# Moving the 1/rms factor of the feed-forward norm behind the gate product, and building the first operands inside the output projection

## The reference

```
h = x + jnp.concatenate([att, y], axis=-1) @ w_out
f = rmsnorm(h, norm_ffn)          # h * (1/rms(h)) * g, 1/rms is one number per token
h = h + (jax.nn.silu(f @ w_gate) * (f @ w_up)) @ w_down
```

## Time and profile before

| | |
|---|---|
| median of 3 runs | 2945.24 us (2944.84 to 2957.09) |
| profiled execution | 2950.53 us, of which the span of the trace is 2948.7 us |
| PE | 2762.0 us busy (94%) |
| DVE | 1696.8 us busy (58%) |
| ACT | 1022.3 us busy (35%) |
| POOL | 391.4 us busy (13%) |
| mean granted TensorE clock | 0.975 |

### The profile page before, as it was taken

One profiled execution on the slowest core, in us unless ns is written; L12 is line 12 of the kernel. 1 busy time (PEld: TensorE's weight loads), 2 busy tenths in 40 slices (PEclk: granted clock), 3 DMA queues, 4 the chain that ended last, 5 costly groups with the idle time before them and its releaser, 6 DMA issues.

```text
span 2948.7 us, 49257 instructions
## 1 busy us (share of the span) xinstructions
PE 2762.0 (94%) x20329; PEld 2628.2 (89%) x20329; DVE 1696.8 (58%) x2517; ACT 1022.3 (35%) x1517; POOL 391.4 (13%) x166
## 2 busy tenths in 40 slices
PE   7999998999999988996899999999999989999997
PEld 7977998877777766995899999999999989999997
DVE  3222699345444445106777777777766787777423
ACT  5233221333323233223433433343344353443222
POOL 2322332211111101341000000000000000000231
PEclk9999999999999998997999999999999999999999
DMA  6322322655555546341334334333432364654521
GB/s 236 95 83 66 102 80 67 167 158 156 149 154 151 155 121 211 126 132 47 102 118 132 119 110 131 126 110 121 136 102 96 128 223 155 222 162 159 197 102 65
DMA packets 394447, 388.80 MB, mean 132 GB/s; under 512 B 25405, under 2 KB 354725, under 8 KB 391160
## 3 DMA queue, kind: packets, MB, share of 16 engines
q1 hardware_dynamic: 367112, 360.00, 38.9%
q10 hardware_dynamic: 27120, 25.77, 2.6%
HBM read 319.11 MB, written 68.00 MB: 131 GB/s over the span
## 4 chain that ended last, share of the span: by engine, by line
PE 72%; issue 14%; DVE 5%; POOL 5%; ACT 2%; DMA 1%; SPq 0%; ACTq 0%; POOLq 0%; DVEq 0%
PE PS L1335 43%; PE PS L890 16%; PE PS L1317 5%; POOL WL L782 4%; PE PS L1085 1%; PE PS L1282 1%; PE PS L1269 1%; PE PS L1056 1%; PE PS L1075 1%; PE PS L1113 1%; DVE xo_t L2466 0%; PE PS L1259 0%; POOL WL L815 0%; PE PS L1102 0%; DMA xin<-in_x_prompt 0%
## 5 line engine op out<-in xcount | busy, mean ns | idle before, releaser
L1335 PE MATMUL PS<-xo_t,WH 128*128 128x288 f32 x2560 | 519.5, 297 | 21.7 <-ACT kept L1745 10.0
L890 PE MATMUL PS<-AH,WH 128*128 128x288 f32 (+1 forms) x2208 | 490.2, 304 | 19.8 <-POOL WL L782 6.4
L890 PE MATMUL PS<-AL,WH 128*128 128x288 f32 (+1 forms) x2208 | 478.7, 299 | 0.0
L890 PE MATMUL PS<-AH,WL 128*128 128x288 f32 (+1 forms) x2208 | 477.6, 298 | 0.0
L1335 PEld LDWEIGHTS PS<-xo_t,WH 128*128 128x128 f32 x2560 | 414.9, 190 | 23.4 <-issue 23.4
L1335 PE MATMUL PS<-xo_x,WH 128*128 128x288 f32 x1920 | 387.2, 296 | 14.7 <-DVE xo_x L2432 14.3
L890 PEld LDWEIGHTS PS<-AH,WH 128*128 128x128 f32 (+1 forms) x2208 | 361.5, 192 | 42.1 <-issue 34.4
L1335 PE MATMUL PS<-xo_t,WL 128*128 128x288 f32 x1280 | 379.6, 297 | 0.0
L890 PEld LDWEIGHTS PS<-AL,WH 128*128 128x128 f32 (+1 forms) x2208 | 361.9, 192 | 0.0
L890 PEld LDWEIGHTS PS<-AH,WL 128*128 128x128 f32 (+1 forms) x2208 | 361.0, 191 | 0.0
L2318 DVE TENSOR_TENSOR WL<-WRAW,WH 128x1024 fp32r<-128x1024 f32 x200 | 244.7, 1224 | 138.7 <-ACT WH L1737 137.6
(11 more groups left out here) (369 smaller groups left out, 3606.1 us busy)
## 6 DMA issues: line engine op xcount, KB each, us to landing
WRAW<-in_w_gate SPq DMA_DIRECT2D x22, 2048.0 KB
WRAW<-in_w_up SPq DMA_DIRECT2D x22, 2048.0 KB
WRAW<-in_w_down SPq DMA_DIRECT2D x32, 1024.0 KB
WRAW<-in_w_in SPq DMA_DIRECT2D x14, 2048.0 KB, 8.3
raw<-in_w_in SPq DMA_DIRECT2D x48, 512.0 KB, 4.1
kca<-in_cache_k SPq DMA_DIRECT2D x256, 64.0 KB, 2.8
vca<-in_cache_v SPq DMA_DIRECT2D x256, 64.0 KB, 2.0
WRAW<-in_w_out SPq DMA_DIRECT2D x16, 1024.0 KB, 10.9
```

Of the source, the lines that this page charges most:

```text
L890: last = nc.tensor.matmul(G[gslot][0:width, h, 0:HALF], wt[:, half if slot is None else slot, k % 8, 0:width], act[:, k, h * HALF:(h + 1) ...
L1335: last = mm(out, wt[:, k, :], act[:, m, k, :], start=(j in (0, 1, 3) and k == 0 and wt is wh and m == 0), stop=(k == 7 and wt is wl), skip ...
```

## The change

- **1/rms.** `XR` is no longer multiplied by 1/rms. The seven products run on h*g. The sums of the gate pair in `gs2` are multiplied by 1/rms before silu (`scale_gate(.., False)`), and the result of silu is multiplied by it again (`scale_gate(.., True)`), which stands for the factor of the up sums. That is four DVE multiplications of 128x576 for each of 22 gate/up couples, placed at the preparation of j = 3 (one), 4 (one) and 5 (two) of the odd pair; `gates` on ACT moves one product later. The sum of squares now accumulates in `rstd` itself. `norm_sum` moves on PE from ahead of product 0 to ahead of product 4, the two roots on ACT behind `cast(6)`, and the reciprocal becomes two of 128x288 on DVE at steps 6 and 7.
- **Operands.** The residual is added in `xt`, which is squared, stored and weighed from there. x00 and the difference t1 are made after tile 8, t3 and t2 tile by tile (`pieces`, two DVE operations of 128x288). The seven operands lie at other addresses, so that x00 can be written while the output projection still reads its own operands. `load_x` on SP now waits for the store, the square and the weighing of tile n-2.
- **Order.** Pair 0 does its products in the order j = 0, 3, 1, 2, 4, 5, 6. The second of the three weight slots is the separate buffer `W3`, so both the first and the second weight operand are made before the last half unit ends.
- **End of the Strassen part.** DVE makes the four low parts `low_hidden(0, 0, j)` ahead of its last two `gather`s, and PE waits for all sums only before the second half of its first down product.

```diff
-              (("x00", low), ("x10", low + SET), ("t1", low + 2 * SET), ("t2", low + 3 * SET), ("x11", high), ("t3", high + SET), ("t4", old))}
+              (("x10", low), ("t2", low + SET), ("t1", low + 2 * SET), ("x11", low + 3 * SET), ("x00", high), ("t3", high + SET), ("t4", old))}
+        acc = rstd[:, :, :].rearrange("p a b -> p (a b)")
+        seq[0:7] = [(0, j) for j in (0, 3, 1, 2, 4, 5, 6)]
             def load_x(n):
                 if n >= 2:
-                    sp.wait_ge(s["tile_taken"], T3 + n - 1)
+                    sp.wait_ge(xr_st[n % 2], 16 * (n // 2))
+                    sp.wait_ge(s["sqf_done"], n - 1)
+                    sp.wait_ge(s["x_g"], n - 1)
-            return WH[:, r, :, :] if r < 2 else W3[:, 0, :, :]
+            return W3[:, 0, :, :] if r == 1 else WH[:, r // 2, :, :]
...
+                    if t and isinstance(c, int) and c == CD:
+                        pe.wait_ge(s["e_add"], 4 * NALL)
-            norm_sum()
             for c, (q, j) in enumerate(seq):
+                if c == 0:
+                    pe.wait_ge(s["tile_taken"], T3 + KT)
+                if c == 4:
+                    norm_sum()
...
-                act.wait_ge(s["e_add"], ADD[2 * p, 6])
                 for t in range(2):
+                    act.wait_ge(s["gate_sc"], 2 * p + t + 1)
                     actv(gs2[:, t, :], gs2[:, t, :], ACT.Silu).then_inc(s["p_silu"], 1)
-                if c % 14 == 8 and c // 14 < NPAIR // 2:
+                if c % 14 == 9 and c // 14 < NPAIR // 2:
                     gates(c // 14)
...
+            def pieces(n):
+                k = n - 8
+                x01, x11 = XR[:, k, HALF:NT], XR[:, n, HALF:NT]
+                dve.wait_ge(s["x_g"], n + 1)
+                tt(x01, x11, x01, ALU.subtract).then_inc(s["x_n"], 1)
+                dve.wait_ge(s["x_n"], 2 * k + 2)
+                tt(XR[:, k, 0:HALF], x01, XR[:, k, 0:HALF], ALU.add).then_inc(s["x_n"], 1)
+            def scale_gate(p, t, again):
+                if again:
+                    dve.wait_ge(s["p_silu"], 2 * p + t + 1)
+                else:
+                    dve.wait_ge(s["ry_done"], 3)
+                    dve.wait_ge(s["e_add"], ADD[2 * p, 6])
+                tt(gs2[:, t, :], gs2[:, t, :], acc, ALU.mult).then_inc(s["silu_sc" if again else "gate_sc"], 1)
...
+                    if c in (6, 7):
+                        given(dve, f"ssf{c - 6}")
+                        nc.vector.reciprocal(rstd[:, c - 6, :], rstd[:, c - 6, :]).then_inc(s["ry_done"], 1)
+                    if q2 % 2 and q2 < NPAIR and j2 in (3, 4, 5):
+                        for t in ((0,), (1,), (0, 1))[j2 - 3]:
+                            scale_gate(q2 // 2, t, j2 == 5)
+                    if c == NPROD - 1:
+                        for j in range(4):
+                            low_hidden(0, 0, j)
```

More of the change, by code:

```diff
@@ L383, in build @@
                 RAW[q, what] = len(RAW) + 1
+        RAW[0, "difference"], RAW[0, "sum"] = RAW[0, "sum"], RAW[0, "difference"]
         assert all(POS[q, 6] == max(POS[q, j] for j in range(7)) for q in range(NALL))
@@ L1763, in _ @@
                     hi_p(C3 + c, c % 4, c // 4)
-                if c % 2 and c >= 3:
-                    n = (c - 3) // 2
-                    squares(n)
-                    if n:
-                        weigh_x(n - 1)
-            cast(0, 0, 0, 0, 0)
-            squares(15)
-            weigh_x(14)
-            cast(1, 0, 1, 1, 0)
+                if c % 2:
+                    squares((c - 3) // 2)
+                    weigh_x((c - 3) // 2)
+                if c == 17:
+                    act.wait_ge(s["x_g"], 8)
+                    x_high("x00", x_part(0, 0))
+            cast(0, 0, 0, 0, 0)
+            cast(1, 0, 3, 1, 0)
+            act.wait_ge(s["w_used"], C3 + 32)
+            act.wait_ge(s["x_n"], 1)
+            x_high("t1", diff[:, :, :])
+            weigh_x(15)
+            cast(2, 0, 1, 2, 0)
+            act.wait_ge(s["x_g"], 16)
+            x_high("x10", x_part(1, 0))
+            squares(15)
+            act.wait_ge(s["x_n"], 17)
+            x_high("t2", x_part(0, 0))
+            keep(0, 0, 0)
+            cast(3, 0, 2, 0, 0)
+            keep(0, 3, 0)
+            act.wait_ge(s["x_lo"], 2)
+            x_high("t3", x_part(0, 1))
+            cast(4, 0, 4, 1, 0)
+            x_high("x11", x_part(1, 1))
+            keep(0, 2, 0)
+            cast(5, 0, 5, 2, 0)
+            act.wait_ge(s["x_n"], 18)
+            act.wait_ge(s["x_lo"], 5)
+            x_high("t4", x_part(1, 0))
+            cast(6, 0, 6, 0, 0)
             for h in range(2):
@@ new lines, in pieces @@
+            def pieces(n):
[5 more added lines that the diff above has]
+                tt(XR[:, k, 0:HALF], x01, XR[:, k, 0:HALF], ALU.add).then_inc(s["x_n"], 1)
+            for n in range(KT):
+                if n:
+                    add_squares(n - 1, "sqf_done", "ssf_used")
+                if n == 9:
+                    x_low("x00", x_part(0, 0), 1)
+                    dve.wait_ge(s["x_lo"], 1)
+                    tt(diff[:, :, :], x_part(0, 1), x_part(0, 0), ALU.subtract).then_inc(s["x_n"], 1)
+                    dve.wait_ge(s["x_n"], 1)
+                if n >= 9:
+                    pieces(n - 1)
+                if n == 15:
+                    dve.wait_ge(w_ld[0], 160)
+                    sum_w(0, 1, 0)
+                    low_w(0, 0, 0, 0)
+                    difference(0, 0)
+                    low_w(1, 3, 1, 0)
@@ L2404, in _ @@
                 dve.wait_ge(xt_in[n % 2], 16 * (n // 2 + 1))
                 dve.wait_ge(s["w_used"], C3 + (2 * n + 2 if n else 3))
-                tt(two(XR[:, n, :]), G[(T3 + n) % 2][:, :, 0:HALF], two(xt[:, n % 2, :]), ALU.add).then_inc(s["tile_taken"], 1)
-                if n:
-                    add_squares(n - 1, "sqf_done", "ssf_used")
-                if n == 14:
-                    low_w(0, 0, 0, 0)
-                    difference(0, 0)
-                    second(0, 2, 0)
-            add_squares(KT - 1, "sqf_done", "ssf_used")
@@ L2416, in _ @@
-            low_w(1, 1, 1, 0)
-            fourth(0, 2, 0)
-            for h in range(2):
-                given(dve, f"ssf{h}")
-            nc.vector.reciprocal(rstd[:, :, :], rstd[:, :, :]).then_inc(s["ry_done"], 1)
-            dve.wait_ge(s["ry_done"], 2)
-            def normed(kh, th):
-                dve.wait_ge(s["x_g"], 8 * kh + 8)
-                v = x_part(kh, th)
-                tt(v, v, rstd[:, th, :].rearrange("p (k t) -> p k t", k=1).to_broadcast([P, 8, HALF]), ALU.mult).then_inc(s["x_n"], 1)
@@ L2453, in _ @@
+                tt(two(x), G[(T3 + n) % 2][:, :, 0:HALF], two(x), ALU.add).then_inc(s["tile_taken"], 1)
+            x_low("t1", diff[:, :, :], 2)
+            low_w(2, 1, 2, 0)
+            pieces(15)
+            x_low("x10", x_part(1, 0), 3)
+            add_squares(15, "sqf_done", "ssf_used")
+            prepare(3, 0, 2, 0, 0, lambda: x_low("t2", x_part(0, 0), 4))
+            dve.wait_ge(s["x_lo"], 3)
             tt(x_part(1, 0), x_part(1, 0), x_part(0, 0), ALU.subtract).then_inc(s["x_n"], 1)
-            prepare(5, 0, 5, 2, 0)
+            for t in range(2):
+                dve.wait_ge(xr_st[t], 16 * (KT // 2))
@@ L2455, in _ @@
+            prepare(4, 0, 4, 1, 0, lambda: x_low("t3", x_part(0, 1), 5))
+            prepare(5, 0, 5, 2, 0, lambda: x_low("x11", x_part(1, 1), 6))
             x_low("t4", x_part(1, 0), 7)
```

98 lines of the change are left out of this document (28 added, 70 removed).

## The result

The changed kernel takes 2923.78 us, the median of seven runs (2917.94 to 2938.63); the kernel before, also in seven runs, takes 2949.82. The ratio is 0.9917, with a 95% interval from 0.9901 to 0.9933: 20 to 29 us faster. The forecast was 2914.3, in a range from 2907 to 2923; so the time lies 0.8 us outside. The seven runs of before have a median 4.6 us above that of the three runs from which the forecast started. That explains nearly half of the 9.5 us between forecast and time, and the rest has to be found in the trace. The profiled execution of the changed kernel has a span of 2922.0 us (before 2948.7).

The account below looks back on a forecast made before the run. PE (94% busy) bounds the kernel, its idle time lying at the joints, mostly ended by DVE. -33.1 + 3.7 + 2.0 - 3.5 = -30.9, so 2945.2 becomes 2914.3 us; range 2907 to 2923.

Parts of the forecast that it names:

- rivals 1 and 2: First: clock falls inside pair 0, time 2921, chance 0.12. Second: each odd pair leaks, time 2925, chance 0.09.
- Joint 1: Between output projection and pair 0's end: shorter DVE chain ends pair 0 at 1387.2 for 1420.3, gain 33.1 us.
- Rival 1: Clock falls inside pair 0: products 3 to 6 take 6.4 us each, pair 0 ends 9.6 us later; 2921, chance 0.12.
- Pair 1: Two reciprocals of 1.9 us come when DVE has no lead; PE waits 0.8, 2.1 and 0.8 us, cost 3.7.
- Later odd pairs: Four more DVE steps of 0.68 us per couple; ACT's `keep` of j = 2 has 1.3 us left, cost nothing.
- rivals 2 and 3: Second: odd pairs leak 0.5 us each, 2925, chance 0.09. Third: multiplications are dear (3.75 us each), 3015, chance 0.02.
- Joint 2: At q = 44, where DVE becomes the bound: last couple's multiplications fall directly ahead, cost 2.0 us, bounds 0 and 4.
- Projection: Inside the output projection: 11.8 us more DVE and a 2.11 us cast find room, cost 0; other end 3.9 us.
- Joint 3: End of the Strassen part: low parts go ahead of two gathers, PE's whole 3.47 us wait goes, gain 3.5 us.
- The base: The median of the runs shown, 5.3 us below the profiled execution: 2945.2 us, from which the forecast time was taken.

Follow-up runs that it names:

- r1: The changed kernel itself run again, beside others on the same chip: 2923.9 us, ratio 0.9917 to the kernel before.
- r2: The changed kernel with the load of the second hidden group ahead of the last store of sums, run again: 2920.98 us, ratio 0.9908.
- e1: The changed kernel with SP's load of the second hidden group issued ahead of the last store of sums: 2916.71 us, ratio 0.9883 to the kernel before.
- e2: The changed kernel with the end of the Strassen part in its old order: 2929.7 us, ratio 0.9923 to the kernel before.
- e6: The changed kernel without the multiplications of gate sums and silu by 1/rms, both reciprocals kept: 2920.74 us, ratio 0.991 to the kernel before.
- e6b: The changed kernel without the four 1/rms multiplications of each couple and without the two reciprocals: 2917.22 us, ratio 0.9878 to the kernel before.
- e7: The changed kernel with the first multiplication of each gate half done twice: 2936.34 us, ratio 0.9956 to the kernel before.
- f3: The changed kernel with the early hidden load, and low parts of three pair 0 weights made by POOL, not DVE: 2917.49 us, ratio 0.9892.

## Why the prediction was off

The forecast's sum was -33.1 + 3.7 + 2.0 - 3.5 = -30.9 on the profiled execution. By the landmarks it is -32.8 + 2.7 + 1.7 + 3.1 = -25.3. Another 0.1 us was lost within the down products, and 1.5 were won ahead of T, which other executions give and take back: -26.7 in all. The median lies at 2923.78, near the 2921 and 2925 of rivals 1 and 2; that is chance, for neither is what happened.

- **Joint 1: right, to 0.3 us.** The forecast took DVE's row at 1420.29 as the end of pair 0 before and PE's end as that after; on PE's rows alone its 33.1 are 32.9, and 32.8 were measured. PE's idle times of 0.6, 1.3, 3.5, 2.9, 0.3 and 1.2 us were forecast. The rows read 0.43, 1.01, 3.25, none, 0.21 and 1.08: the 2.9 were filled by a product that ran slow (4.8 us for 3.2) and by the norm's sums. The window there (busy PE, PEld, DVE, ACT, POOL, then the granted clock) shows the lower level, 1.2 GHz:

```profile
1368.00:1370.00 2.00, 1.66 (x7) 1.69 (x8) 2.00 (x2) 1.78 (x1) 0.00 (x0) 0.50 0.01 4
```

  Rival 1, the clock, thus held for one product of seven and cost nothing, because DVE was the bound. In r1, r2, e1 and e2 it fell in pair 1 as well (a window there reads 0.50), where a product took up to 4.99 us and 0.9 were lost.
- **Pair 1: 2.7 for 3.7, the mechanism right.** Waits of 0.8, 2.1 and 0.8 us were forecast; the first did not come, the others read 1.72 and 0.47. e6 and e6b show that the reciprocals are 2.0 of the 2.7.
- **Later odd pairs: right with the cost nothing**; rivals 2 and 3 are dead, a multiplication taking 0.75 us. But the room was 0.96 us and not 1.3 (e7).
- **Joint 2: 1.7 for 2.0, right** (e6: 1.8).
- **Projection: right that it is free.** Tiles are 12.80 us apart before and after. How it is free was wrong: see the last section. The 5.3 us for POOL's instruction do not follow from the row either: by 0.23 us for 0.37 it would have been 6.3, and PE 1.1 us late.
- **Joint 3: the step that failed.** The text says: "so all of the wait goes. Gain 3.5 us". The wait went, and the gain was -3.1, 6.6 us off with the wrong sign. The step looked at the row in which PE waited and at what DVE needed to remove it, but not at what would be late next, which the other steps asked. Rows for it stood in the trace of before: ACT idle for 5.91 us for `hraw`, and POOL's weights ready only 1.5 us ahead of PE, which was held up by 5.0. Had it been asked, the step would have read 1.5. From there to -3.1 it is that the load lands 20.8 us after the last product and not 18.6 (SP's issue takes 1.18 us for 0.47, and the flight is longer), and that PE, having stood still for 5.68 us, starts on the slow clock (4 matmuls in 1.33 us for 0.69). Why the load was slower is not shown; among the kernels with the load behind the store it lands at 18.5 to 21.0 us.
- **The base: 4.6 us.** The median of three runs lay under the median of seven, and the range, which took in the far bounds of the steps, had nothing for this.

From the later base the forecast would have been 2918.9, and a range moved up by the same 4.6 us would have held 2923.78; with joint 3 at 1.5 as well it would have been 2920.9. The 2.9 us that are left are the slower load and the slow matmuls behind it, less what pair 1 and joint 2 cost less than forecast, and the spread of the runs.

## What to carry to other kernels

When a wait is removed, look at what the engine will ask for next and how long before that it became ready. If this is less than what is removed, the rest comes back as the next wait. Here there were 1.5 us of room for 5.0 us of wait and slow clock, and the new wait, 5.68 us for 3.47 and with more slow matmuls behind it, cost more than the old one. A load that an engine must cast in order ahead of the next weights should be issued ahead of a store that is due at the same moment, if nothing waits for the store as early (e1: the load is there at 13.2 us and not at 20.8). And work moved from a busy DVE to an idle POOL is not off DVE when both read two tensors in SBUF (f3).
